# Weight-tile splits redistributed over the blocks of the last stage's first chunk

## What is computed

```
def _merge(x, oa, za, ob, zb, ga, gb, gate, w_br_a, w_br_b, w_out):
    ya = (oa * jax.nn.silu(za)) @ w_br_a
    yb = (ob * jax.nn.silu(zb)) @ w_br_b
    h = jax.nn.sigmoid(ga) * ya + jax.nn.sigmoid(gb) * yb
    return x + gate * (h @ w_out)
...
y_sample = _rmsnorm(xs) * final_norm_g
```

## Time and profile before

| | |
|---|---|
| time, median of 3 runs | 1214.87 us (1214.77 to 1215.3) |
| the profiled execution's own time | 1214.08 us |
| its span | 1212.3 us |
| TensorE busy (matmuls) | 1187.5 us, 98% of the span |
| VectorE busy | 819.3 us, 68% |
| ScalarE busy | 601.3 us, 50% |
| GpSimd busy | 92.4 us, 8% |
| first chunk of the last stage | about 976 to 1024 us |

### The profile page before, as it was taken

The page is one execution under the profiler, slowest core; times in us unless marked ns, Lnnn a source line. Parts: engine busy times, 40 slices in busy tenths (PEclk is TensorE's granted clock), DMA queues, the critical chain, the costliest instruction groups (busy, mean ns, idle before and its releaser), DMA issues.

```text
span 1212.3 us, 19668 instructions
## 1 busy us (share of the span) xinstructions
PE 1187.5 (98%) x7432; PEld 1076.8 (89%) x7432; DVE 819.3 (68%) x1596; ACT 601.3 (50%) x1205; POOL 92.4 (8%) x108
## 2 busy tenths in 40 slices
PE   7999999999999999999999999999999999999998
PEld 1799889989998998899899899989989988998996
DVE  4769458656765776587687597688779966454453
ACT  4632335535552654365465455555547675344342
POOL 0000000000000000000000000000000034533430
PEclk9999999999999999999999999999999999999999
DMA  9547702141123215022511121411113376642540
GB/s 362 178 175 226 231 30 72 45 135 61 40 79 96 64 40 162 22 72 69 139 63 46 49 63 41 134 39 58 38 40 124 113 233 211 204 152 95 201 146 35
DMA packets 71762, 132.81 MB, mean 110 GB/s; under 512 B 6774, under 2 KB 47734, under 8 KB 71676
## 3 DMA queue, kind: packets, MB, share of 16 engines
q1 hardware_dynamic: 57420, 109.70, 28.0%
q10 hardware_dynamic: 14256, 21.96, 5.0%
HBM read 96.24 MB, written 35.40 MB: 109 GB/s over the span
## 4 chain that ended last, share of the span: by engine, by line
PE 84%; DVE 9%; ACT 3%; issue 2%; DMA 1%; POOL 0%; ACTq 0%; SPq 0%; DVEq 0%
PE d_ps_pairs L84 23%; PE s_ps_pairs L84 12%; PE y_ps L1881 9%; PE o_ps_pairs L1070 9%; PE b_ps L84 8%; PE t_ps_pairs L1040 7%; PE v_ps L84 6%; PE s_ps_pairs L1004 4%; PE s_ps_pairs L1003 4%; DMA wada<-in_w_ada 1%; DVE pt L1401 1%; PE k_ps L352 1%; DVE mn L1407 1%; PE t_ps L344 1%; DVE q L1392 1%
## 5 line engine op out<-in xcount | busy, mean ns | idle before, releaser
L84 PE MATMUL d_ps_pairs<-h,wt 128*128 128x384 f32 (+2 forms) x1920 | 352.2, 338 | 0.9 <-ACT craw L1212 0.9
L84 PEld LDWEIGHTS d_ps_pairs<-h,wt 128*128 128x128 f32 x1920 | 316.7, 189 | 16.4 <-ACT craw L1212 1.9
L1401 DVE TENSOR_TENSOR pt<-t_ps_pairs,pt 128x512 fp32r<-128x512 f32 (+2 forms) x264 | 152.9, 619 | 64.7 <-ACT pt L1170 63.5
L84 PE MATMUL s_ps_pairs<-h,wt 128*128 128x512 f32 (+1 forms) x864 | 168.2, 354 | 0.0
L84 PEld LDWEIGHTS s_ps_pairs<-h,wt 128*128 128x128 f32 x864 | 141.6, 189 | 21.7
L1170 ACT ACTIVATE pt<-t_ps_pairs 128x512 fp32r<-128x512 f32 (+2 forms) x264 | 130.2, 544 | 16.8 <-PE t_ps_pairs L1040 11.5
L1194 ACT ACTIVATE pr<-s_ps_pairs,mx 128x896 f32<-128x896 f32 (+1 forms) x128 | 125.0, 982 | 26.9 <-DVE mx L1429 26.5
L1040 PE MATMUL t_ps_pairs<-ident_sb,pr 128*128 128x128 f32 x928 | 125.6, 274 | 1.9 <-DVE pt L1401 1.1
L1881 PE MATMUL y_ps<-wo,mg 128*128 128x512 f32 (+1 forms) x504 | 113.2, 385 | 0.0
L1040 PEld LDWEIGHTS t_ps_pairs<-ident_sb,pr 128*128 128x128 f32 x928 | 105.4, 140 | 8.8 <-DVE pt L1401 5.8
L1881 PEld LDWEIGHTS y_ps<-wo,mg 128*128 128x128 f32 x504 | 91.3, 188 | 20.6
(11 more groups left out here) (204 smaller groups left out, 1588.0 us busy)
## 6 DMA issues: line engine op xcount, KB each, us to landing
wraw<-in_w_gate SPq DMA_DIRECT2D x24, 512.0 KB, 3.8
gt<-gates_d SPq DMA_DIRECT2D x40, 256.0 KB, 4.5
gates_d<-craw ACTq DMA_DIRECT2D x48, 192.0 KB, 1.9
v_d<-vst SPq DMA_DIRECT2D x20, 320.0 KB, 4.6
wada<-in_w_ada SPq DMA_DIRECT2D x12, 512.0 KB, 9.8
oz<-gates_d SPq DMA_DIRECT2D x20, 256.0 KB, 4.6
oz<-o_d SPq DMA_DIRECT2D x20, 256.0 KB, 4.3
x_f<-in_x SPq DMA_DIRECT2D x10, 512.0 KB, 7.0
```

The lines of the kernel that those rows point to most:

```text
L84: mm = eng.matmul(out, lhs(a, k), rhs(b, k), start=(k == 0 and i == 0), stop=(k == n_k - 1 and i == 2))
L1401: dve.tensor_tensor(pt[:, 1, c * 512:c * 512 + cols], t_ps[:, n % 2, 0:cols], pt[:, 0, c * 512:c * 512 + cols].bitcast(F32), ALU.subtract) ...
```

## The change

One line of numbers in `finish` differs. It says which tiles are split in which block of the first chunk, on ScalarE and on VectorE alike.

```
@@ def finish(...)
     ALL = 2 * PAIRS
     HALF = NU // 2
 
-    EXTRA = [[4], [5, 6], [7], [8, 9], [10], [11, 12], [13], [14, 15]]
+    EXTRA = [[4], [5], [6], [7, 8], [9], [10, 11], [12, 13], [14, 15]]
     TAIL = [slice(0, 512), slice(512, 768), slice(768, 1024)]
```

## The result

| | before | changed |
|---|---|---|
| median | 1214.77 us (9 runs, 1213.2 to 1215.3) | 1219.49 us (9 runs, 1217.64 to 1221.26) |
| ratio | | 1.0044, 95% interval 1.0035 to 1.0052 |
| profiled execution, own time / span | 1214.08 / 1212.3 us | 1221.15 / 1219.3 us |

The change makes the kernel 4.7 us slower by the medians, and 0.44% slower by the ratio (the medians alone would give 0.39%). The profiled execution took 1221.15 us, 1.7 above the median; a second profile of the same kernel, in the experiments, has 1216.45. Both are needed, since they differ in a way that matters. One execution of a kernel in the experiments (the one with all but tile 12 moved) took 1299.57 us at a mean granted clock of 0.851 and is left out of its ratio.

The account below looks back on a forecast made before the run. TensorE bounds the kernel, busy in all 156 us after the first chunk. Chain + 4.3 us and clock + 0.2 us on the profiled 1214.08 give 1218.6; with the median 0.8 above the profiled run, 1219.4, range 1216.9 to 1221.4.

Parts of the forecast that it names:

- Block 4's stall goes: First chunk: tp(2) no longer runs behind low(6), so TensorE finds block 4 ready at 987.97; gain 1.10 us.
- Blocks 6 and 7: First chunk: block 6 starts at about 995.15 (due 993.73), block 7 waits some 0.5 us for tp(5); gain left 0.2 us.
- The gate-load chain: First chunk: high(10) behind sig(6) delays gate load 7, then sig(7), low(12), y(4) and mglow(7); TensorE 4.3 us later.
- L6 + L7: Landing times of gate loads 6 and 7 in the first chunk, from issue to sigmoid start; sum kept at 9.5 us.
- The clock: TensorE's idle 3.5 us ahead of y(4) may drop its clock from 2.4 to 1.2 GHz; 0.2 us added.
- Nothing later gives it back: From 1024 to 1180 TensorE is busy in all of the 156 us, so a first-chunk delay moves the end equally.
- L6 + L7 - 5.2: How much later TensorE gets at y(7), from mglow(7) ending at 1006.3 + L6 + L7 against 1011.46; 4.3 us.
- The estimate by the Trainium skill: About 2.0 us plus bytes over 436 GB/s per transfer: L6 + L7 is 6.9, shift 1.7 us; within a 12% rival.
- the shortest pair: In the rival of a faster kernel (6%): L6 + L7 must be below 5.2 for any gain, shortest pair shown 6.6.

Follow-up runs that it names:

- the load-order experiments: Changed kernel with all first-chunk gate loads issued ahead of the weight loads: ratio 0.9986; the kernel before with the same: 1.0002; changed with gate load 7 alone first: 1.0022.
- the filled kernels: Changed kernel with 14 added matmuls ahead of y(4): ratios 1.0035 and 1.0044; kernel with only tiles 6 and 7 moved, 12 added ahead of block 6: 1.0007.

## Why the prediction was right

The forecast was 1219.4 us and the median is 1219.49. The mechanism was right; that the two agree within 0.1 us is luck. Step by step:

- *Block 4's stall goes:* right, 96 matmuls in one piece.
- *Blocks 6 and 7:* right in kind. Block 6 was expected at 1.4 us past its due time and came at 0.9 (994.87, against 982.41 + 11.52 = 993.93), since gate load 4 landed in 5.5 us and low(8) ended 0.4 us early (the stage had started 0.2 us late). Block 7 was put at 0.5 and came at 1.3 (999.02, due at 997.75): gate load 5 took 5.6 us, and low(9), behind sig(5), was late. The output product starts at 1001.96, 0.3 us later than before and not 0.2 earlier. In the second profile the two stalls are 0.4 and 0.7 us, and it starts 18.51 us behind block 2 (999.80 - 981.29), 0.9 us sooner than before (1001.62 - 982.21 = 19.41).
- *The gate-load chain:* right, with its fixed parts nearly exact. From sig(6) to gate load 7, 3.24 us for 3.2; from sig(7) to y(4), 2.98 for 2.9. In the sum L6 + L7 the total was about right and the parts were not: 6.41 + 4.10 = 10.5 in the first profile, 5.36 + 3.88 = 9.2 in the second, for 9.5. The reason given (gate load 6 with w(11) close ahead, gate load 7 with w(13) far ahead) is the one that the parts bear out.
- *The clock:* the size was off. The term of 0.2 us rested on a fall of 3.4 us. In the first profile it lasted 6.8 us and cost 1.75; in the second it didn't come. As a mean over both it would be nearer 0.9.
- *Nothing later gives it back:* right, 156 of 156 us. (The vector work behind mglow(7) moves by 1015.8 - 1010.67 = 5.1 us in the prediction's own terms, not 5.5; nothing hangs on it.)

In the second profile the chunk grew by 3.28 us over the kernel before, less than the 4.0 that L6 + L7 - 5.2 gives with 9.24. In the first it grew by 6.80, of which 1.75 are the clock's, and 5.05 are left where the formula gives 5.3 with 10.51. So the constant is too small, by 0.3 us there and by 0.8 in the second: low(8), and with it gate load 6, came 0.4 and 0.9 us earlier behind block 2 than worked out. Errors of opposite sign met, a chain put some tenths too long and a clock term too small. Neither profile is near the forecast's 4.5 by itself, and no trace was taken of a run at the median, so how the two errors balance there is not shown. The mechanism is shown by the load-order experiments.

The estimate by the Trainium skill, DMA: Bandwidth & Descriptors (Anatomy of one DMA), by which the shift would have been 1.7 us, was not borne out: no pair of landings with SP's queue as in the kernel before was under 8.2 us in these profiles, where the estimate was 6.9. The 6.6 that the prediction calls the shortest pair is twice the shortest single landing of 3.3 us and not a pair that was seen.

What the prediction did not see is how the loss is shared. It put nearly all of it on tiles 10 and 12. Moved alone they cost 0.23%, and tiles 6 and 7 alone 0.13 to 0.16%; both traces of the latter show one stall of about 2 us where there were two of about 1, with a fall of the clock behind it. What share of the 0.44% the clock has in the mean stays open within the bound above: the filled kernels did not separate it from the spread of the landings (L6 was 5.1 to 7.6 us in the four profiles of the changed kernel and its filled version).

## What to carry to other kernels

When work is moved later on an engine, follow what its completion releases on the DMA queue, and then what stands behind that load in the queue: here a split that nobody needed yet freed a staging buffer, the load for that buffer stood in front of a gate load, and the gates were what TensorE needed. Put loads that depend on nothing near the front of the queue before spreading the work that releases the others; either edit alone was worth nothing or less, both together were 0.14% faster than the kernel before. And in these traces two waits of TensorE of 1 us cost less than one of 2, which brought the slow clock with it.

## What the runs showed of the hardware

- In the first chunk, a wait of TensorE of about 2 us was followed by a fall of the granted clock from 2.4 to 1.2 GHz, 1.0 to 1.4 us after the work had begun again: three profiles (waits of 1.88, 1.96 and 2.44 us), each with 3.4 us at 1.2 GHz and 1.5 to 1.6 us lost. Yet a wait of 3.05 us there brought no fall, and one of 3.78 us a fall of 6.8 us. The waits of up to 1.67 us in this chunk brought none.
- The length of the wait alone does not decide it. All fourteen profiles have the same wait of 1.26 us ahead of 37.5 to 38.1 us; in nine the clock falls between 0.1 us ahead of its end and 2.1 us behind it, for 3.4 us, and in five it does not. All have one wait ahead of 21.1 to 21.6 us too: of 1.37 to 2.67 us in thirteen of them, with no fall behind it, and of 2.98 us in the other, with one.
- The Trainium skill, TensorE: Matmul & The Clock Gate (Why this matters for your kernels), warns against idle gaps above a certain length between bursts of matmuls. The waits of 1.88 to 2.44 us are below that length and had a fall behind them, so staying below it is no safe ground here.
- A gate load of 256 KB took 3.9 to 4.1 us to land as gate load 7 of the changed and the filled kernel, with one 512 KB load issued just ahead of it and the load before that one 4.7 us earlier or more. As gate load 6 of the same kernels it took 5.1 to 7.6 us, with two 512 KB loads issued in the 2.1 us before it.
